# Two transformer blocks on one core: the pooling mixer by token tiles, two weight remainders on GpSimd, and the first products in another order

## The reference, cut to what matters

```python
qkv = rms_norm(x, norm_mix[0]) @ attn_w_qkv           # the first products
...
x = x + squared_relu_mlp(rms_norm(x, norm_mlp[0]), mlp_w_up[0], mlp_w_down[0])   # MLP 0
xn = rms_norm(x, norm_mix[1])
# group g (256 channels): mean over the last (2, 4, 8, 16)[g] tokens, minus the token
pooled = (c[:, 1:] - lower) / count - xn
y = einsum('bsgc,gcd->bsgd', pooled, pool_w) * pool_scale
x = x + y
x = x + squared_relu_mlp(rms_norm(x, norm_mlp[1]), mlp_w_up[1], mlp_w_down[1])   # MLP 1
```

## Time and profile before

| what | value |
|---|---|
| median of 3 runs | 1082.19 us (1080.5 to 1082.43) |
| profiled execution | 1080.91 us |
| its span, first to last instruction | 1078.7 us, mean granted TensorE clock 0.998 |
| TensorE busy | 1064.9 us (99%) |
| VectorE, ScalarE, GpSimd busy | 739.5, 564.0, 40.7 us |

### The profile page before, as it was taken

One profiled execution on the slowest core, in us unless ns is written; L12 is line 12 of the kernel. 1 busy time (PEld: TensorE's weight loads), 2 busy tenths in 40 slices (PEclk: granted clock), 3 DMA queues, 4 the chain that ended last, 5 costly groups with the idle time before them and its releaser, 6 DMA issues.

```text
span 1078.7 us, 15297 instructions
## 1 busy us (share of the span) xinstructions
PE 1064.9 (99%) x5800; PEld 907.2 (84%) x5800; DVE 739.5 (69%) x1053; ACT 564.0 (52%) x737; POOL 40.7 (4%) x61
## 2 busy tenths in 40 slices
PE   8999999999999999999999999999999999999997
PEld 7788888888888888888888888888889778888886
DVE  6756765656686556468887876566897879566665
ACT  6556534444455344346675554455654766444453
POOL 1000000000000000000000310000300200000000
PEclk9999999999999999999999999999999999999999
DMA  9953375564547565636543765656576225665651
GB/s 348 335 162 117 105 233 188 176 211 158 183 132 244 194 194 166 223 107 204 178 130 105 231 198 159 215 177 228 166 260 221 69 78 171 219 194 159 209 177 39
DMA packets 127164, 195.83 MB, mean 182 GB/s; under 512 B 6978, under 2 KB 97218, under 8 KB 126995
## 3 DMA queue, kind: packets, MB, share of 16 engines
q1 hardware_dynamic: 123904, 185.77, 52.1%
q0 software_dynamic: 3216, 9.51, 2.9%
q10 hardware_dynamic: 2, 0.00, 0.0%
HBM read 194.21 MB, written 1.05 MB: 181 GB/s over the span
## 4 chain that ended last, share of the span: by engine, by line
PE 91%; DVE 5%; ACT 2%; DMA 1%; issue 1%; SPq 0%; DVEq 0%; ACTq 0%
PE ps L2133 26%; PE ps L2028 15%; PE ps L2030 14%; PE ps L2029 14%; PE ps L2136 13%; PE ps L2215 1%; DMA raw<-attn_w_qkv_in 1%; PE ps L2288 1%; PE ps L2059 1%; DVE wlo L1134 1%; ACT whi L681 1%; PE ps L2314 1%; PE ps L2230 1%; DVE act L1259 1%; PE ps L2728 1%
## 5 line engine op out<-in xcount | busy, mean ns | idle before, releaser
L2133 PE MATMUL ps<-act,whi 128*128 128x512 f32 x1200 | 424.7, 397 | 0.1
L1134 DVE TENSOR_TENSOR wlo<-raw,whi 128x2048 fp32r<-128x2048 f32 (+2 forms) x161 | 363.9, 2276 | 87.7 <-ACT whi L681 87.4
L2136 PE MATMUL ps<-act,wlo 128*128 128x256 f32 x1200 | 336.6, 280 | 0.0
L681 ACT ACTIVATE whi<-raw 128x2048 fp32r<-128x2048 f32 (+2 forms) x170 | 317.6, 1887 | 27.1 <-PE ps L2030 21.6
L2133 PEld LDWEIGHTS ps<-act,whi 128*128 128x128 f32 x1200 | 225.3, 188 | 54.3 <-issue 0.2
L2136 PEld LDWEIGHTS ps<-act,wlo 128*128 128x128 f32 x1200 | 226.7, 189 | 2.0
L2030 PE MATMUL ps<-whi,hlo 128*128 128x512 f32 x400 | 157.3, 393 | 0.0
L2029 PE MATMUL ps<-wlo,hhi 128*128 128x512 f32 x400 | 156.7, 392 | 0.0
L2028 PE MATMUL ps<-whi,hhi 128*128 128x512 f32 x400 | 156.3, 391 | 0.0
L2028 PE MATMUL ps<-whi,act 128*128 128x512 f32 (+2 forms) x270 | 106.1, 393 | 1.5 <-DVE arena L1693 0.6
L2030 PE MATMUL ps<-whi,act 128*128 128x512 f32 (+2 forms) x270 | 101.8, 377 | 0.0
(11 more groups left out here) (245 smaller groups left out, 1150.1 us busy)
## 6 DMA issues: line engine op xcount, KB each, us to landing
raw<-mlp_w_up_in SPq DMA_DIRECT2D x32, 1024.0 KB, 6.4
raw<-mlp_w_down_in SPq DMA_DIRECT2D x32, 1024.0 KB, 4.9
raw<-ffn_w_gate_in SPq DMA_DIRECT2D x22, 1024.0 KB, 5.4
raw<-ffn_w_up_in SPq DMA_DIRECT2D x22, 1024.0 KB, 5.4
raw<-ffn_w_down_in SPq DMA_DIRECT2D x22, 1024.0 KB, 4.9
raw<-attn_w_qkv_in SPq DMA_DIRECT2D x10, 1024.0 KB, 9.5
raw<-w_kv_shared_in SPq DMA_DIRECT2D x8, 1024.0 KB, 5.3
raw<-attn_w_o_in SPq DMA_DIRECT2D x4, 1024.0 KB, 5.2
```

Source lines behind the costliest of these rows:

```text
L681: nc.scalar.activation(whi[:, s, 0:width], raw[:, s, 0:width], ACT.Copy).then_inc(hi_ready, 1)
L1134: nc.vector.tensor_tensor(wlo[:, s, 0:width], raw[:, s, 0:width], whi[:, s, 0:width].bitcast(F32), ALU.subtract).then_inc(lo_ready, 1)
L2133: nc.tensor.matmul(bank(b + f), lhsT=w[0][:, at:at + P], rhs=act[:, k, :, :].rearrange("p a t -> p (a t)"), start=k == 0, stop=False, skip ...
L2136: ins = nc.tensor.matmul(bank(b + f, 0, T), lhsT=w[1][:, at:at + P], rhs=act_hi[:, k, :], start=False, stop=k == KT - 1, skip_group_check= ...
```

## The change

1. **Order at the start.** TensorE fills without a pause until the first products. Quarters 1 and 3 are turned inside `first_products(0, 0)`, and its six pairs of products are reordered. ScalarE and VectorE convert chunk 4 before the sine and cosine instead of after them.
2. **Two remainders move to GpSimd**: those of the pooling chunk and of the first chunk of MLP 1, each one subtraction of 128 x 2048. GpSimd also multiplies the first two quarters of MLP 1's input by the gain.
3. **Pooling by tiles.** Tile 0 is pooled before unit 6 of tile 1 in `last_downs`. The pooling weights then multiply tile 0 (two parts) before tile 1 is pooled. The band of each tile is scaled half on ScalarE and half on VectorE. The turned quarters of MLP 1 get four banks instead of two. `copy_pooled(p)` on ScalarE and `split_pooled(p)` on VectorE split a pooled quarter of 128 x 512 as L988 and L1779 do before, and `add_pooled(p)` adds a finished part to x.

```diff
# GpSimd
+            def remainder(c):
+                s = SLOT[c]
+                pool.wait_ge(hi_ready, c + 1)
+                pool.wait_ge(lo_ready, c)
+                nc.gpsimd.tensor_tensor(wlo[:, s, :], raw[:, s, :], whi[:, s, :].bitcast(F32), ALU.subtract)\
+                    .then_inc(lo_ready, 1)
             for name in ROWS[1:ROW["fpost0"] + 1]:
+                if name == "final":
+                    remainder(AT["pool"])
+                    remainder(AT["mlp1"])
+                    wait_row(pool, "mlp1")
+                    first_gained("mlp1", 0)
+                    first_gained("mlp1", 1)
                 load_row(name)
# (first_gained: waits for x_ready of quarter p, then xs = x * row over 128x512, on GpSimd)
# ScalarE
             stats("mix0")
+            hi_before(1)
...
                     sum_squares("mix1", t, x[:, t, h * HALF:(h + 1) * HALF], HALF, h)
+                    if t == 1 and h == 0:
+                        copy_pooled(0)
+                        copy_pooled(1)
                 root("mix1", t)
+                act.wait_ge(scale_ready, 4 + 2 * t)
+                nc.scalar.activation(scaled(band, t), scaled(const_band, t), ACT.Copy,
+                                     scale=norm_stat("mix1", t, 6)).then_inc((band_first, band_second)[t], 1)
+            copy_pooled(2)
+            copy_pooled(3)
+            copy_turned("mlp1", (0, 1))
+            hi_next()
+            copy_turned("mlp1", (2, 3))
             hi_before(AT["pool"])
# VectorE
-                lo_before(n0 + 2 * (NM - 1) - 1)
+                if last:
+                    lo_before(n0 + 2 * (NM - 1) - 1)
...
+            lo_before(1)
             dve.wait_ge(trig_ready, 2)
...
+                def scaled_band(t):
+                    link(newton(t))
+                    dve.sem_inc(scale_ready, 2)
+                    lo, hi = ((0, P + 16), (T, 3 * P))[t]
+                    nc.vector.tensor_scalar(band[:, 2:4, lo:hi], const_band[:, 2:4, lo:hi], st(t, 6), None, ALU.mult)\
+                        .then_inc((band_first, band_second)[t], 1)
+
                 add(0)
+                add(1)
                 gained("mix1", 0)
-                add(1)
+                variance(0)
                 gained("mix1", 1)
-                variance(0)
-                newton(0).then_inc(scale_ready, 2)
+                scaled_band(0)
                 add(2)
                 gained("mix1", 2)
+                split_pooled(0)
+                split_pooled(1)
                 add(3)
                 gained("mix1", 3)
                 release_row()
                 variance(1)
+                scaled_band(1)
...
+            add_pooled(0)
+            add_pooled(1)
+            split_pooled(2)
+            split_pooled(3)
+            split_turned("mlp1", (0,))
+            add_pooled(2)
+            wait_row(dve, "mlp1")
+            dve.wait_ge(xs_ready, 4 * XSR["mlp1"] + 2)
+            gained("mlp1", 2)
+            split_turned("mlp1", (1,))
+            add_pooled(3)
+            gained("mlp1", 3)
+            split_turned("mlp1", (2, 3))
# TensorE
+            def pooled_tokens(t):
+                lo, hi = ((0, P + 16), (T, 3 * P))[t]
+                for kk in range(KT):
+                    if kk % 4 == 0:
+                        pe.wait_ge(xs_ready, 4 * XSR["mix1"] + 2 * t + kk // 4 + 1)
+                    if kk == 0:
+                        pe.wait_ge((band_first, band_second)[t], 2)
+                    o = bank(4 + kk // 2, (kk % 2) * T + t * P, (kk % 2) * T + (T if t else P + 16))
+                    ins = nc.tensor.matmul(o, lhsT=xs[:, t, kk * P:(kk + 1) * P], rhs=band[:, kk // 2, lo:hi],
+                                           start=t == 0 and kk % 2 == 0, stop=t == 1, skip_group_check=True)
+                    if kk % 4 == 3:
+                        ins.then_inc(pooled, 1)
...
+                            if f is mlp[0] and u == 6:
+                                pe.wait_ge(masks_loaded, 16)
+                                pooled_tokens(0)
                             ins = unit(n, k, 1, half)
...
             turn_x(2)
-            fill(3)
-            turn_x(1)
-            fill(6)
+            fill(9)
...
                 two(0, act_hi, hi, start=c == 0)
+                if c == 0 and h == 0:
+                    turn_x(1)
                 pe.wait_ge(act_lo_ready, 2 * c + 1)
                 two(0, act_lo, hi)
+                pe.wait_ge(*((lo_ready, c + 1) if h else ((first_half_lo, second_half_lo)[c], 1)))
+                two(0, act_hi, lo, stop=c == 1)
+                if c == 0 and h == 0:
+                    turn_x(3)
                 pe.wait_ge(act_hi_ready, 2 * c + 2)
                 two(1, act_hi, hi, start=c == 0)
...
+            for p in range(4):
+                t, h = p // 2, p % 2
+                if p == 2:
+                    pooled_tokens(1)
+                wait_acts("mix1", p + 1)
                 for g in (2 * h, 2 * h + 1):
                     for k in range(2):
                         ins = product(bank(p, (g % 2) * FC, (g % 2 + 1) * FC),
...
+                    if p == 2 and g == 0:
+                        turn("mlp1", parts=(0,))
+                ins.then_inc(*((pool_part, 1) if p < 3 else (w_used, 1)))
+                if p == 2:
+                    turn("mlp1", parts=(1,))
```

More of the change, by code:

```diff
@@ L363, in turned_bank @@
         def turned_bank(name, p):
+            if name == "mlp1":
+                return p
             return 4 + (p % 2 if name in SPLIT_ENTRY else p)
@@ L1768, in pool_entry, with split_pooled, add_pooled @@
                 variance(1)
[L1769 to L1772, removed]
+                scaled_band(1)
+            def split_pooled(p):
+                dve.wait_ge(act_hi_ready, 4 * ACTN["mix1"] + p + 1)
+                t, h = p // 2, p % 2
+                cols = (slice(4 * h, 4 * h + 4), slice(t * P, (t + 1) * P))
+                nc.vector.tensor_tensor(act_lo[:, cols[0], cols[1]], pooled_quarter(p),
+                                        act_hi[:, cols[0], cols[1]].bitcast(F32), ALU.subtract).then_inc(act_lo_ready, 1)
+            def add_pooled(p):
+                h, t, cols = quarter("mlp1", p)
+                dve.wait_ge(*((pool_part, p + 1) if p < 3 else (w_used, AT["pool"] + 1)))
+                nc.vector.tensor_tensor(x[:, t, cols], x[:, t, cols], bank(p), ALU.add).then_inc(x_ready, 1)
             mlp_layer(mlp[0], scale_pool_weights)
             pool_entry()
[L1776 to L1782, removed]
+            add_pooled(0)
[11 more added lines that the diff above has]
+            split_turned("mlp1", (2, 3))
+            cursor[0] = AT["mlp1"] + 1
+            dve.wait_ge(lo_ready, AT["mlp1"] + 1)
             lo_before(mlp[0].first + 31)
@@ L2559, in _ @@
             mlp_layer(mlp[0], "mlp0", TILES, True)
-            pe.wait_ge(masks_loaded, 16)
-            for t in range(TT):
-                lo, hi = ((0, P + 16), (T, 3 * P))[t]
-                pe.wait_ge(xs_ready, 4 * XSR["mix1"] + 2 * t + 2)
-                pe.wait_ge(*((band_second, 2) if t else (band_first, 1)))
-                for kk in range(KT):
-                    o = bank(4 + kk // 2, (kk % 2) * T + t * P, (kk % 2) * T + (T if t else P + 16))
-                    ins = nc.tensor.matmul(o, lhsT=xs[:, t, kk * P:(kk + 1) * P], rhs=band[:, kk // 2, lo:hi],
-                                           start=t == 0 and kk % 2 == 0, stop=t == 1, skip_group_check=True)
-                    if t and kk % 2:
-                        ins.then_inc(pooled, 1)
             c = AT["pool"]
             wait_chunk(c + 1)
-            for n, (h, t) in enumerate(TILES):
+            for p in range(4):
+                t, h = p // 2, p % 2
+                if p == 2:
+                    pooled_tokens(1)
+                wait_acts("mix1", p + 1)
                 for g in (2 * h, 2 * h + 1):
-                    wait_acts("mix1", g + 1)
                     for k in range(2):
-                        ins = product(bank(2 * t + h, (g % 2) * FC, (g % 2 + 1) * FC),
+                        ins = product(bank(p, (g % 2) * FC, (g % 2 + 1) * FC),
                                       acts(2 * g + k, t * P, (t + 1) * P),
@@ L2582, in _ @@
                                       start=k == 0, stop=k == 1)
-                ins.then_inc(pool_part if n < 3 else w_used, 1)
-                if n >= 2:
-                    turn("mlp1", parts=(n - 2,))
+                    if p == 2 and g == 0:
[3 more added lines that the diff above has]
+                    turn("mlp1", parts=(1,))
             mlp_layer(mlp[1], "mlp1", QUARTERS)
```

31 lines of the change are left out of this document (16 added, 15 removed).

## The result

The changed kernel takes 1086.26 us (median of six runs, 1085.19 to 1087.51), the kernel before 1081.60 in six runs beside it (1080.5 to 1082.43). The ratio is 1.0046, with an interval of [1.0036, 1.0056]: slower by 4.7 us, between 3.9 and 6.1. The forecast was 1086.8, +4.6 on a median of 1082.2 for the kernel before, which in these six runs is 0.6 lower. The profiled execution took 1085.81 us with a span of 1083.9, against 1080.91 and 1078.7 before.

What follows compares the result with a forecast made beforehand. TensorE was taken as the bound, busy 1064.9 of 1078.7 us. The terms -1.3 + 3.85 + 3.0 - 0.9 gave +4.6 on a median of 1082.2, so 1086.8 us, range 1081.6 to 1090.5.

Steps and rivals of the forecast that it cites:

- The start: First products begin 1.2 us sooner, of which 0.6 stays, and the gap at 33.37 goes (-0.7): -1.3 us.
- The first remainder: End of MLP 0: GpSimd's subtraction for the pooling chunk holds VectorE's L1542, so TensorE comes 3.85 us later.
- the sign: What would show it right: L1542 drawn out to about 4 us, TensorE waiting 3.9 us at 289 for L1500.
- The second remainder: GpSimd's subtraction for MLP 1's first chunk holds `gained(0)`; TensorE waits 3.0 us for the band of tile 0.
- Rival four: The two gaps drop TensorE's clock to half: +3 us on top of the forecast, 1089.8; chance 7%.
- Pooling by tiles: Between MLP 0 and MLP 1: waits around pooling tile 1 shrink by 0.7, MLP 1's entry by 0.2: -0.9 us.
- I look for nothing later.: Behind 318 us both programs are the same and TensorE sets their pace, so no further shift.
- One: Rival: GpSimd's work does not slow VectorE; -2.2 us, 1080.0; chance 10%.
- two: Rival: GpSimd and VectorE share the port in proportion; -0.2 us, 1082.0, no change; chance 12%.
- Three: Rival: only the first remainder costs time, the second does not; +1.6 us, 1083.8; chance 7%.

Runs made afterwards that it cites:

- both_dve: Changed kernel with both weight remainders back on VectorE, the second in two halves; GpSimd keeps only the two gains; 1080.27 us, 0.9995 of the kernel before.
- kept_busy: Changed kernel with seven idle identity products issued by TensorE ahead of its wait for the last hidden block; 1087.93 us, 1.0058 of the kernel before.
- tiles_only: `in_halves` with the order at the start as in the kernel before; 1080.07 us, 0.9989 of the kernel before.
- one_left: Changed kernel with the pooling chunk's remainder back on VectorE, that of MLP 1's first chunk left on GpSimd; 1085.35 us, 1.0040 of the kernel before.
- first_only: Changed kernel with the pooling chunk's remainder left on GpSimd, that of MLP 1's first chunk back on VectorE; 1084.85 us, 1.0042 of the kernel before.
- in_halves: Changed kernel with remainders on VectorE, the pooling chunk's in halves, and ScalarE's square sum of MLP 1's tile 0 earlier; 1078.77 us, 0.9984; again 1079.56, 0.9988.
- four_pieces: Changed kernel with each of GpSimd's two subtractions of 128 x 2048 cut into four of 128 x 512; 1085.19 us, 1.0040 of the kernel before.
- only_writes: Changed kernel with both remainders on VectorE and eleven GpSimd memsets of a scratch tile in the first subtraction's place; 1080.01 us in a single execution.

## Why the prediction was right, point by point

**The start, -1.3.** Measured -1.43 in the trace: 0.47 by the second chunk (21.70 to 21.23, forecast 0.6), the rest with the gap at 33.37, which is gone. First products begin at 8.94, as said. That trace is the best of twelve, though; six of them gain only 0.1 to 0.5, and in medians the term is worth -0.6 to -1.2. That it agrees so well in the profile is luck.

**The first remainder, +3.85.** Measured +3.74, and as the sign asked, L1585 (L1542 before) at 4.16 us. The subtraction took 4.56 (4.5 by the multiplications of the earlier trace rows), L1585 stood until GpSimd's end, and `both_dve`, which takes both remainders off GpSimd, has neither the 4.16 nor the wait. The whole of it rested on one reading, that L1562 in the earlier trace rows ends with GpSimd and that L1552, with PSUM, does not care.

**The second remainder, +3.0.** The size is right, 2.8, and 2.74 where the clock is whole (`kept_busy`). What TensorE did with the time was not as I wrote it. I let it run at full speed from the first gap to the second; it ran at half for twelve products, arrived at the pooling 2.1 us later and waited 0.7, so the wait of 3 us that was to show it is not in the trace. VectorE's additions were late with it, so `gained(0)` was held for 1.98 and not the 3.5 of the forecast.

**Rival four, the clock.** I gave it 7% as +3 on top. The clock did fall behind the first gap, to 0.50, but it cost nothing on top. My own sentence had the reason, that the second gap swallows it, and still let 3 of 4.2 us through: the products up to unit 6 did not all run at half speed, only twelve of them, 2.14 us, less than the 2.7 of cover. Where the clock fell without cover, it cost: 1.6 us in `kept_busy`. The Trainium skill (TensorE: Matmul & The Clock Gate, Part 1), by which the clock falls to half after idle time, had the direction right, and this trace now shows it.

**Pooling by tiles, -0.9.** The table has -1.18 between the pooling of tile 0 and MLP 1, the two runs without a remainder on GpSimd -0.73 for the whole stage, and -1.0 in medians for `tiles_only`. The other 0.5 belongs to the second remainder: with it off VectorE, tile 1's pooling to the first product of MLP 1 takes 13.76 us in the changed kernel and 13.77 in `one_left`, against 14.30 in `both_dve` and 14.26 in `first_only`. The prediction had no such gain. The bare wait before tile 1 is 0.68 (0.9 forecast), the one for its split 0.52 (0.5 forecast).

**"I look for nothing later."** This was wrong by 0.5. Behind 318 ScalarE rounds a chunk at 318.20 before it sums the squares of MLP 1's input:

```profile
318.20 1.91 ACT L710 ACTIVATE whi<-raw 128x2048 fp32r<-128x2048 f32 x1
320.00 1.05 ACT L745 ACTIVATE junk<-x 128x1024 f32<-128x1024 f32 x1
```

VectorE waits 1.26 us for that sum (L1214 at 322.49 above), makes the first remainder of a hidden block (L1537) at 327.37, and TensorE waits 0.3 for it. The code is the same as before, but `add_pooled(3)` now comes closer to MLP 1's entry, and the order on ScalarE puts 1.9 us in between. I had compared the programs and not the distances. `both_dve` has the same 0.6 there, and `in_halves`, where ScalarE sums the squares of tile 0 before that rounding, has none.

**The other rivals.** One (GpSimd costs nothing) and two (a share) are refuted by L1585 at 4.16 and by the operations of about 1 us in `four_pieces`, and `only_writes` shows what GpSimd may do beside VectorE at no cost. Three (only the first hurts) is refuted by the 4.20 of `gained(0)` in `kept_busy` and by `one_left`, where the second alone costs +4.3.

The errors of the terms are -0.1, -0.1, -0.2 and -0.3 (the tiles bring 0.2 less than forecast, the freed VectorE 0.5 more) and +0.5 for the late remainder of MLP 1; they nearly cancel. With the scatter behind 600 us the trace ends at +5.2, and the weaker start in most executions brings the median back to +4.7. The mechanism and the size of the two remainders were right, the way in which TensorE would spend the second was not, and the sum is closer to the measured +4.7 than its parts deserve.

## What to carry to other kernels

Before moving an elementwise operation to an idle GpSimd, list what VectorE runs in that time with two SBUF inputs, and ask which of it the path needs: a subtraction of 4.6 us that saved VectorE 2.28 cost TensorE 3.7. Cutting it into pieces spreads the standing over more operations (1.0040 of the time before, against 1.0046), it does not remove it; halving it on VectorE around the urgent chain did (0.9984).

Costs of gaps don't add: a half clock between two waits of the same chain is free here, and taking away one of two such losses returns much less than its price alone (+4.0 and +4.1 us in the stage for either, +5.4 for both). Compare such kernels by a stage in the traces: there the same code repeats to 0.01 us, where medians leave 1 us open. And where an edit brings an engine's last step closer to the next stage, read that stage's queue order again even if its code is unchanged.

## What the runs showed of the hardware that was not expected

- VectorE operations on a single column (128 x 1, two SBUF inputs) also stand for a GpSimd subtraction: 1.07 and 1.21 us instead of 0.16 to 0.22.
- The granted clock of TensorE fell in or behind gaps of 3.78, 3.64, 2.74 and 2.07 us, and stayed whole behind the 1.64 of the earlier trace rows and the pair of 1.03 and 1.13. Fourteen idle instructions in 3.18 us kept it whole across the first gap. Behind the same wait of 3.78 us the half clock lasted for twelve products in the changed kernel and for six in `first_only`.
- A GpSimd subtraction of 128 x 2048 took 4.55 to 4.63 us in every kernel; cut in four and among VectorE's steps, 5.56 and 6.00.
